# Order of the two attentions in the first block: banded heads projected first, banded items queued behind the dilated projections

## The reference

```python
h = rmsnorm(x, ln1_g[l])
proj = h @ w_in[l]
qa, ka, va, qb, kb, vb, ga, gb = jnp.split(proj, offsets, axis=-1)
qa = apply_partial_rope(rmsnorm(qa.reshape(B, S, DIL_HEADS, HEAD_DIM), q_norm_a[l]), cos, sin)
ka = apply_partial_rope(rmsnorm(ka.reshape(B, S, DIL_HEADS, HEAD_DIM), k_norm_a[l]), cos, sin)
oa = dilated_attention(qa, ka, va)
qb = apply_partial_rope(rmsnorm(qb.reshape(B, S, SWA_Q_HEADS, HEAD_DIM), q_norm_b[l]), cos, sin)
kb = apply_partial_rope(rmsnorm(kb.reshape(B, S, SWA_KV_HEADS, HEAD_DIM), k_norm_b[l]), cos, sin)
ob, _ = banded_attention(qb[:, None], kb[:, None], vb[:, None], SWA_WINDOW - 1, sinks[l])
mix = jax.nn.sigmoid(ga) * (oa @ w_branch_a[l]) + jax.nn.sigmoid(gb) * (ob @ w_branch_b[l])
x = x + mix @ w_out[l]
```

## Time and profile before

| | us |
|---|---|
| median of 3 runs | 2494.79 (2494.7 to 2498.89) |
| the profiled execution, its own time | 2495.9 |
| its span in the trace | 2494.1 |
| PE busy in it | 2430.4 |

### The profile page before, as it was taken

The page is one execution under the profiler, slowest core; times in us unless marked ns, Lnnn a source line. Parts: engine busy times, 40 slices in busy tenths (PEclk is TensorE's granted clock), DMA queues, the critical chain, the costliest instruction groups (busy, mean ns, idle before and its releaser), DMA issues. The chain is left out here.

```text
span 2494.1 us, 29035 instructions
## 1 busy us (share of the span) xinstructions
PE 2430.4 (97%) x11174; PEld 1949.3 (78%) x11174; DVE 1215.6 (49%) x1937; ACT 928.0 (37%) x1447; POOL 1314.1 (53%) x1593
## 2 busy tenths in 40 slices
PE   8999979999999999999899999999999989999999
PEld 7776758888888888776687888888887767788887
DVE  4778656433224532359734843333324796266431
ACT  4454443322224223454524442332325454344321
POOL 4645326665556655445345665555553462456554
PEclk9999989999999999999999999999999999999999
DMA  4211113333333333212122333333332211223333
GB/s 174 83 51 56 56 51 93 97 98 95 100 96 111 93 100 101 76 59 63 49 68 85 94 101 93 102 93 94 101 99 60 68 59 43 88 82 99 96 97 98
DMA packets 59609, 213.37 MB, mean 86 GB/s; under 512 B 6608, under 2 KB 6736, under 8 KB 59344
## 3 DMA queue, kind: packets, MB, share of 16 engines
q1 hardware_dynamic: 59472, 211.52, 27.8%
HBM read 209.39 MB, written 2.10 MB: 85 GB/s over the span
## 5 line engine op out<-in xcount | busy, mean ns | idle before, releaser
L664 PE MATMUL banks<-t,t 128*128 128x512 f32 (+5 forms) x10854 | 2399.3, 390 | 34.4 <-POOL t L1842 16.4
L664 PEld LDWEIGHTS banks<-t,t 128*128 128x128 f32 (+1 forms) x10854 | 1912.4, 189 | 497.1 <-issue 84.5
L1842 POOL TENSOR_TENSOR t<-t,t 128x256 fp32r<-128x256 f32 x1548 | 1260.1, 846 | 1148.8 <-ACT t L1579 1148.8
L1579 ACT ACTIVATE t<-t 128x1024 fp32r<-128x1024 f32 x387 | 410.1, 1060 | 1152.2 <-issue 584.1
L1118 DVE TENSOR_TENSOR t<-banks,t 128x512 f32<-128x512 f32 x121 | 83.3, 689 | 205.8 <-PE banks L664 205.7
L1285 DVE TENSOR_TENSOR t<-banks,t 128x512 f32<-128x512 f32 x44 | 30.4, 691 | 183.6 <-PE banks L664 183.5
L1253 DVE SCALAR_TENSOR_TENSOR t<-banks,t 128x512 f32<-128x512 f32 x32 | 22.1, 692 | 155.4 <-PE banks L664 155.4
L1006 DVE SCALAR_TENSOR_TENSOR t<-t,t,t 128x512 fp32r<-128x512 f32 x64 | 51.5, 805 | 61.1 <-ACT t L1588 61.1
L1230 DVE TENSOR_TENSOR t<-t,t 128x512 fp32r<-128x512 f32 x68 | 70.1, 1030 | 2.3
L1259 DVE TENSOR_TENSOR t<-banks,t 128x512 f32<-128x512 f32 x24 | 16.6, 692 | 106.0 <-PE banks L664 106.0
L1280 DVE TENSOR_TENSOR t<-banks,t 128x512 f32<-128x512 f32 x44 | 30.4, 691 | 70.3 <-PE banks L664 69.9
(11 more groups left out here) (160 smaller groups left out, 1235.7 us busy)
## 6 DMA issues: line engine op xcount, KB each, us to landing
t<-in_w SPq DMA_DIRECT2D x387, 512.0 KB, 3.5
t<-in_xT SPq DMA_DIRECT2D x8, 256.0 KB, 5.4
out<-t SPq DMA_DIRECT2D x8, 256.0 KB, 4.6
t<-in_dmask SPq DMA_DIRECT2D x1, 1536.0 KB, 11.3
t<-in_vbias SPq DMA_DIRECT2D x2, 384.0 KB, 4.1
t<-in_c SPq DMA_DIRECT2D x1, 576.0 KB, 7.9
t<-in_pos SPq DMA_DIRECT2D x2, 256.0 KB, 5.8
t<-in_smask SPq DMA_DIRECT2D x1, 256.0 KB, 11.4
```

Of the source, the lines that this page charges most:

```text
L664: return pe.matmul(o, l, r, start=start, stop=stop, skip_group_check=True)
L1579: a.activation(whl[u % 2][:, 0:1024], wraw[u % 3][:, :], ACT.Copy).then_inc(*w_high.next(u))
L1842: p.tensor_tensor(hl[:, 1024:2048][:, c], wraw[u % 3][:, c], as_f32(hl[:, c]), ALU.subtract).then_inc(*w_low.next((u, q)))
```

## The change

The plan of weights and the projections have kb and qb ahead of the dilated tiles. The banded outputs get tiles that nothing else uses at this time (86, 106 and 108 KB, and a part of `vb_t`), and the waits for `dil_out` fall away in `swa_item` and `swa_out`. `head1` projects and puts the chain at the head of `waiting`. Behind each of the twelve dilated projections one banded item is put at the end of the queue (`AFTER`); the four items of dilated group 0 are put there behind tile 4, those of group 1 behind the last chain, and the last four banded items behind those. The wait ahead of gates 2 to 10 now names the heads qa 5 and ka 5. `held` gives the planner, for the first item that follows a chain in a slot, the two DVE steps that release the chain's banks (in the second block's `mla_item` too).

```diff
--- before.py
+++ after.py
@@ -55,13 +55,13 @@
     for kt in K8:
         for c0 in range(1792, 2304, 128):
             full("vs", "w_in", 0, [kt], c0)
-    for t in (0, 2, 4, 1, 3, 5):
-        full("qa", "w_in", 0, K8, 128 * t)
-        full("ka", "w_in", 0, K8, 768 + 128 * t)
     full("kb", "w_in", 0, K8, 2816)
     for i in range(4):
         for kt in K8:
             put("qb", "w_in", 0, [(128 * kt, 128)], [(2304 + 64 * i, 0, 64), (2304 + 64 * (4 + i), 64, 64)])
+    for t in (0, 2, 4, 1, 3, 5):
+        full("qa", "w_in", 0, K8, 128 * t)
+        full("ka", "w_in", 0, K8, 768 + 128 * t)
     for m in range(16):
         full("ga" if m < 8 else "gb", "w_in", 0, K8, 3072 + 128 * m)
     for m in range(8):
@@ -563,7 +563,7 @@
         KBt = reg(66, S)[:, :]
         VB = reg(68, 512)[:, :].rearrange("p (c n) -> p c n", c=4)
         OA = [reg(82 + 2 * i, S)[:, :] for i in range(2)]
-        OB = [reg(22 + 2 * i, S)[:, :] for i in range(4)]
+        OB = [reg(86, S)[:, :], reg(106, S)[:, :], reg(108, S)[:, :], vb_t[:, 0:S]]
 
         reg_S = [[reg(88 + 6 * s + 3 * hf, 768)[:, :] for hf in range(2)] for s in range(3)]
         HLA = [reg(o, 1024, F32R) for o in (58, 62, 40, 44, 48, 52)]
@@ -1211,9 +1211,6 @@
 
             def swa_out(i, b):
                 need.wait_ge(*t_attn.at(("swa_values", i, b)))
-                for t in range(2):
-                    for r in range(4):
-                        need.wait_ge(*a_attn.at(("dil_out", t, r)))
                 v.tensor_copy(OB[i][:, 128 * b:128 * b + 128],
                               B[pair(swa_at[i, b][0])[0]][:, 0:128]).then_inc(*v_attn.next(("swa_out", i, b)))
 
@@ -1922,6 +1919,7 @@
                 k["slot"] = slot
                 k["before"] = slot_head.get(slot)
                 slot_head[slot] = (p_attn, ("head", hid))
+                held[slot] = (v_attn, ("summed", hid)), (v_attn, ("turned", hid))
                 yield "av", *k["src"], *k["rope"]
                 put("head_in", hid)
                 yield "t", *k["src"], k["const"]
@@ -1938,6 +1936,8 @@
             return gen
 
         slot_head = {}
+
+        held = {}
 
         def proj(tag, s, dst, after=(), bias=None, scale=1.0):
             b = sch.bank()
@@ -1980,6 +1980,7 @@
         put("values1_strided")
         sch.set_slots(3)
         sch.set_banks([0, 1])
+        AFTER = 1
         rope1 = ((a_norm, ("cos", 1)),)
 
         slot_busy = {s_: [(v_norm, ("rstd", 0))] for s_ in range(3)}
@@ -1987,7 +1988,7 @@
 
         def dil_item(t, r):
             def gen(slot):
-                yield "t", *[(p_attn, ("head", (n, 2 * g + t))) for g in range(3) for n in ("qa", "ka")], *slot_busy[slot]
+                yield "t", *[(p_attn, ("head", (n, 2 * g + t))) for g in range(3) for n in ("qa", "ka")], *slot_busy[slot], *held.pop(slot, ())
                 dil_at[t, r] = slot, slot_busy[slot]
                 slot_busy[slot] = [(a_attn, ("dil_out", t, r))]
                 put("dil_scores", t, r, 0)
@@ -2018,8 +2019,7 @@
 
         def swa_item(i, b):
             def gen(slot):
-                yield ("t", (p_attn, ("head", ("qb", i))), (p_attn, ("head", ("kb", 0))),
-                       *[(a_attn, ("dil_out", t, r)) for t in range(2) for r in range(4)], *slot_busy[slot])
+                yield "t", (p_attn, ("head", ("qb", i))), (p_attn, ("head", ("kb", 0))), (v_evac, ("vn", 3)), *slot_busy[slot], *held.pop(slot, ())
                 swa_at[i, b] = slot, slot_busy[slot]
                 slot_busy[slot] = [(v_attn, ("swa_out", i, b))]
                 put("swa_scores", i, b)
@@ -2037,35 +2037,33 @@
                 put("swa_out", i, b)
             return gen
 
+        def head1(n, t_, R):
+            src = proj(n, 0, R, rope1)
+            sch.waiting.insert(0, head_chain((n, t_), R=R, g=col(n), turn=PG[n], ones=C["bones"], n=64,
+                                                      tiles=slot_tiles, src=[src], const=(v_norm, ("turns1",)), rope=rope1))
+
+        head1("kb", 0, KBt)
+        for i in range(4):
+            head1("qb", i, QB[i])
+        banded = [swa_item(i, b) for b in range(4) for i in range(4)]
         for t_ in (0, 2, 4, 1, 3, 5):
-            if t_ == 1:
+            for n, R in (("qa", QA[t_]), ("ka", KA[t_])):
+                head1(n, t_, R)
+                sch.waiting += banded[:AFTER]
+                del banded[:AFTER]
+            if t_ == 4:
                 for r_ in range(4):
                     sch.waiting.append(dil_item(0, r_))
-            src = proj("qa", 0, QA[t_], rope1)
-            sch.waiting.append(head_chain(("qa", t_), R=QA[t_], g=col("qa"), turn=PG["qa"], ones=C["bones"], n=64,
-                                          tiles=slot_tiles, src=[src], const=(v_norm, ("turns1",)), rope=rope1))
-            src = proj("ka", 0, KA[t_], rope1)
-            sch.waiting.append(head_chain(("ka", t_), R=KA[t_], g=col("ka"), turn=PG["ka"], ones=C["bones"], n=64,
-                                          tiles=slot_tiles, src=[src], const=(v_norm, ("turns1",)), rope=rope1))
-
-        src = proj("kb", 0, KBt, rope1)
-        sch.waiting.append(head_chain(("kb", 0), R=KBt, g=col("kb"), turn=PG["kb"], ones=C["bones"], n=64,
-                                      tiles=slot_tiles, src=[src], const=(v_norm, ("turns1",)), rope=rope1))
-        for i in range(4):
-            src = proj("qb", 0, QB[i], rope1)
-            sch.waiting.append(head_chain(("qb", i), R=QB[i], g=col("qb"), turn=PG["qb"], ones=C["bones"], n=64,
-                                          tiles=slot_tiles, src=[src], const=(v_norm, ("turns1",)), rope=rope1))
         for r_ in range(4):
             sch.waiting.append(dil_item(1, r_))
-        for b in range(4):
-            for i in range(4):
-                sch.waiting.append(swa_item(i, b))
+        sch.waiting += banded
+
         def gate1(k, after=()):
             gates1[k] = proj("ga" if k < 8 else "gb", 0, G1[GATE1[k]], after)
 
         for k in range(2):
             gate1(k)
-        sch.until(("kb", 0), *[("qb", i) for i in range(4)])
+        sch.until(("ka", 5), ("qa", 5))
         heads_done = tuple(slot_head.values())
         for k in range(2, 11):
             gate1(k, heads_done)
@@ -2359,7 +2357,7 @@
             def mla_item(t, b):
                 def gen(slot):
                     yield ("t", *[(p_attn, ("head", (n, l, 2 * t + hf))) for n in ("mq", "mk") for hf in range(2)],
-                           *mla_busy[slot])
+                           *mla_busy[slot], *held.pop(slot, ()))
                     mla_at[l, t, b] = slot, mla_busy[slot]
                     mla_busy[slot] = ((v_attn, ("mla_out", l, t, b)),)
                     put("mla_scores", l, t, b)
```

## The result

The changed kernel takes 2480.05 us in the median of four runs (2479.0 to 2481.86), the kernel before, in the same set of runs, 2494.74 us. The ratio is 0.9939 (95% interval 0.9921 to 0.9956): 14.7 us less, where 11.8 had been forecast. The profiled execution took 2479.0 us.

A forecast was written before the change was run, and what follows sets the result against it. It took PE, busy 97%, as the bound, so only its idle and lower clock count: 21.8 - 5 - 4 - 1 = 11.8 us less, 2484.1 profiled or 2483.0 against the median; range 2478 to 2487, with neighbours 2473 to 2493.

The forecast's parts named there:

- What could be won: First block's attention: PE idle 12.3 us and lower clock 5.6 late, idle 3.9 at 205 to 225 us; ceiling 21.8 us.
- Ahead of gate 11: PE idle before gate 11, which waits for all dilated outputs: 5 us, bounds 0 and 20.
- The cover calculation: Compares PE's end of gate 10, at 312 us, with DVE's pace through attention: DVE 1 to 7 us late.
- Late DVE among the projections: Small PE idle pieces while chains and banded items load DVE under the projections: 4 us, bounds 1 and 8.
- Drain: Gates 11 to 13, 16.3 us of cover for two to four banded items: 1 us idle, bounds 0 and 5.
- `held` in the second block: Second block's attention: tokens may move a matmul group by a step, bounds -1 and +1 us.
- Small pieces of idle and the clock: PE idle in small pieces among work should cost no clock, as with 3.9 us at 205 to 225 us.
- SP's queue and POOL's: Same 387 weight loads in another order; neither SP nor POOL has more to do before any group.
- The shared port: VectorE and GpSimd lock each other out: 2.9 us more DVE, time 2486 if all of it reached PE.
- The signs: After-profile if right: banded softmax near 105 us, no idle piece over 3 us before the drain, last banded copy 335 to 345.
- One sign of being wrong: One long wait ahead of gate 11 for the dilated output or dilated softmax (L1166), with a clock under 1.00.
- The slower rival: Dilated items become the tail ahead of gate 11, which comes 26 us late; 2506 us, chance 9%.

The follow-up runs named there:

- experiment 4: The changed kernel with AFTER = 0, all sixteen banded items behind the dilated ones: 2491.08 us, ratio 0.9975.
- experiment 12: The kernel of experiment 8, with attention in the first block moved forward only after every fourth row block of a projection: 2515.96 us, ratio 1.0077.
- experiment 8: The changed kernel with dilated group 1 queued ahead of the banded items still waiting: 2476.9 us, ratio 0.9911.
- experiment 9: The changed kernel with group 1 queued ahead of waiting banded items and gates 11 to 13 waiting for dilated group 0 alone: 2476.27 us, ratio 0.9917.
- experiment 1: The changed kernel without the `held` tokens in the second block's attention items: 2486.87 us, ratio 0.9959.
- experiment 10: The changed kernel with head chains put at the end of the queue instead of at its head: 2496.31 us, ratio 0.9998.
- experiment 2: The kernel before, with `held` added and used in the second block's attention alone: 2490.69 us, ratio 0.9977.
- experiment 3: The kernel before, with banded outputs on tiles of their own and no wait for dilated outputs, order untouched: 2492.44 us, ratio 0.9981.
- experiment 7: The changed kernel with AFTER = 2, two banded items behind each dilated projection until all sixteen are queued: 2493.11 us, ratio 0.9983.
- experiment 6: The changed kernel with tiles of gates 11 to 15 reordered, so gates 11 to 13 wait for dilated group 0 alone: 2475.75 us, ratio 0.9911.
- experiment 11: The changed kernel without the `held` tokens in the first block's items: 2474.81 us, ratio 0.9915.

## Why the prediction was right

The median of 2480.05 us lies 2.95 under the forecast of 2483 and inside its range. The main mechanism was the one described: banded items under the projections take the tail away (experiment 4 puts most of it back), and what is new stands ahead of gate 11. That the size came out so well is partly luck. In the first block two errors cancel, 4.1 us of PE's own work put at nothing and 3.8 us too much for late DVE; and the second block brings time that had not been expected. By its own steps:

- *What could be won, 21.8 us.* The terms for idle and clock were right: 17.25 us idle and 5.0 lost to the clock between matmul 200 and 1800, 0.9 of it the wait in front of the merge that both kernels have. But the ceiling assumed PE's own work to stay equal by count. It grew by 4.1 us (table of experiment 12), so the most that orders of this kind gave was 16.9 us, in experiments 8 and 9. The mixing is what hides the idle, and it isn't free.
- *Ahead of gate 11, 5 us.* Measured 4.3 us of idle and 1.5 of clock. The cover calculation put the end of gate 10 at 312 us and the dilated outputs 5 to 7 us later; they were at 306.7 and 319.9, 13.2 us apart. DVE's pace was as assumed, 87% busy among the chains (95 to 210 us) and 71% behind. But more attention was still open at gate 10 than the two banded items counted, four banded and two dilated outputs, and PE was busy with it for 8.9 of the 13.2 us. The place was right, and the 5 us nearly; the lateness behind it was about double. The text said that the clock would stay at 1.00; it fell here in both profiles of the changed kernel, and not in experiment 1 behind the same waits.
- *Late DVE among the projections, 4 us.* Measured 0.2 (L815, once). This term was mis-sized. It carried the old 3.9 us of 205 to 225 us over by length, and these were not DVE's lateness but a want of cover: with gates 0 and 1 used up, `until` stood for chains. Chains at the head of the queue removed that, and experiment 10, with the same DVE work and the chains at the end, puts 14.6 us back.
- *Drain, 1 us.* Measured 0.
- *The first block in sum.* Forecast 11.8, measured 11.3: 21.8 less 4.1 for PE's own work, less 4.3 + 1.5 + 0.2 for what was new, is 11.7. The working adds up, with one slip in a reading: it says that two of the four waits of L815 stand in the earlier trace rows, where there are three.
- *`held` in the second block, between -1 and +1.* Wrong: 5 to 7 us faster (experiments 1 and 2). The rows for it were in the trace, two waits for L1022 of 1.3 us with the clock at its lower level around them, but the prediction read PE's waits in the first block alone. Without this part the change gives 9.7 us by the medians (experiment 1), 2.1 under the forecast; with it 14.7, 2.9 over.
- *Small pieces of idle and the clock.* The prediction took the four pieces of 205 to 225 us as a sign that small pieces cost no clock. Experiment 3 has the same four pieces with a fall of 3.4 us behind them. The trace of before was one outcome of two.
- *SP's queue and POOL's* (weights in another order): no wait of PE for POOL between 60 and 360 us, as said.
- *The shared port* of the Trainium skill ("SBUF — State Buffer", section "SBUF: two separate sides"), estimated at 2.9 us more on DVE by its rule: the median of L1209 is 0.35 us in both, and DVE's busy time in the part went from 229.8 to 231.6 us, less than that estimate. Among the projections no lateness of DVE reached PE; whether these 1.7 us had a share in the wait ahead of gate 11 isn't shown.
- *The signs.* Right were the start of banded softmax (106.3 us), no piece of idle over 3 us, and dilated scores of group 1 behind 240 us (268.6). The last banded copy (333.2 us) and PE's waits (5.4 us) lie just under what was named. One sign of being wrong came in a small form: a wait for L1166 ahead of gate 11, 1.3 us, with the clock at 0.86.
- *The slower rival* (9%) wasn't the outcome, but its mechanism is real: experiment 7 has it, at a part of -3.0 us, and experiment 10 the same loss at another place.

The edits don't simply add. Tiles alone give 6.4 us of the part, tiles and banded heads first with all banded items last 2.4 (with `held`, which costs some 4 to 5 us in the full order), the full order 11.3, and the same with `held` left out of this part 16.5. Three kernels are faster than the changed one: experiments 6, 8 and 11 at 2475 to 2477 us, each of whose runs lies under every run of the changed kernel. Their intervals overlap; none is shown to be best, and leaving `held` out together with either of the other edits wasn't tried.

What stays open: how much of the extra work of PE belongs to which kind of boundary; how much of the second block's 5 to 7 us is the waits and how much the clock behind them; and whether the falls of the clock that come elsewhere in the second block belong to the change.

## What to carry to other kernels

When a busy engine has a tail with nothing beside it, count the filler that may legally run up to each barrier, not the filler in all: here the barrier for tiles ahead of gate 11 cost 4 to 6 us, and giving the three gates other tiles removed it. Ask what stands alone in its slots at the end of each class of work and queue something of another class behind it; one item more behind each projection (experiment 7) turns the gain into a loss. And a token that a planner waits for should be tried for each part by itself: the same one saved some 3 us in each layer's attention and cost 4 to 5 in the first block.

## What the runs showed of the hardware that had not been expected

The same waits on the same matmuls can bring a fall of TensorE's clock in one execution and none in another. Three pieces of idle of 2.2, 1.3 and 0.8 us within 11 us, 4.3 us in all, came with a granted clock of 0.86 from 308 to 320 us in the changed kernel, with a like fall in its second profile, and with 1.00 in experiment 1. Four pieces, 3.9 us within 14 us, came with 1.00 from 205 to 225 us before and with 0.91 in experiment 3. Each such fall to the 1.2 GHz level lasted some 3.4 us and cost up to 1.7. In the second block they come at the same few matmuls, most of them during a wait or within 2 us of its end, in some kernels and not in others. So a difference of under 3 us between two profiled executions of whole kernels says little, and even inside the part one fall can stand for 1.5 us of it.
